# Second block's attention as one stage per layer: centred values, early rotation, gate logarithms under the retention, scores a head ahead

## The reference

```python
def retention_inputs(parts, rotate):            # 4 heads of 128
    q = to_heads(parts[0], 4) * 128 ** -0.5; k = to_heads(parts[1], 4)
    if rotate: q, k = rotary_2d(q, ...), rotary_2d(k, ...)      # latent tokens only
    v = to_heads(parts[2], 4)
    # one decay per head and direction: log1p(-exp(ret_decay))
def gla_inputs(parts):                          # 4 heads, keys of 64, values of 128
    a_f = log_sigmoid(parts[8] @ gate_up[0] + gate_b[0]) / 16   # a_b alike, with index 1

r_lat, r_ctx = bidirectional_scan(retention_inputs(lat, True), retention_inputs(cx, False))
g_lat, g_ctx = bidirectional_scan(gla_inputs(lat), gla_inputs(cx))
ret = from_heads(head_layernorm(r)) * silu(parts[3])   # minus mean, over root of variance, per head
gla = from_heads(rmsnorm(g, gla_norm_g)) * silu(parts[7])
x = x + g1 * (concatenate([ret, gla]) @ w_out)
```

## Time and profile before

| | |
|---|---|
| median of 3 runs | 2334.02 us (2332.15 to 2335.29) |
| profiled execution, its own time | 2339.86 us |
| span of the profiled execution | 2338.0 us |
| PE busy | 2096.0 us, 90% of the span |
| DVE, ACT, POOL busy | 707.7, 617.7, 267.7 us |
| granted TensorE clock, mean | 0.938 of full |

### The profile page before, as it was taken

How to read it: one execution, slowest core, us unless ns; L and a number is a source line. 1 busy time by engine, 2 the same in 40 slices (tenths; PEclk the granted TensorE clock), 3 DMA queues, 4 the chain that set the end, 5 groups by cost and what they waited for, 6 DMA issues and landing times. The chain is left out here.

```text
span 2338.0 us, 27789 instructions
## 1 busy us (share of the span) xinstructions
PE 2096.0 (90%) x11630; PEld 1465.7 (63%) x11630; DVE 707.7 (30%) x1250; ACT 617.7 (26%) x968; POOL 267.7 (11%) x121
## 2 busy tenths in 40 slices
PE   5999989989999999979975598999999797568998
PEld 2456787774444444458853446777777686358998
DVE  1103154222222222262333413222222533343333
ACT  1313112022222222231112314223332211334544
POOL 1000000010000000000000012323332000012663
PEclk9999978989999999989988699999999998769999
DMA  9276815257999999922230003343453134003441
GB/s 358 87 256 236 322 37 197 81 219 300 426 424 426 422 420 425 397 104 101 80 137 0 1 27 126 126 162 126 144 189 118 37 120 171 0 1 139 166 163 55
DMA packets 120207, 428.28 MB, mean 183 GB/s; under 512 B 5690, under 2 KB 23141, under 8 KB 107456
## 3 DMA queue, kind: packets, MB, share of 16 engines
q1 hardware_dynamic: 118016, 416.56, 46.4%
q0 software_dynamic: 2112, 10.56, 1.3%
HBM read 426.06 MB, written 1.05 MB: 183 GB/s over the span
## 5 line engine op out<-in xcount | busy, mean ns | idle before, releaser
L490 PE MATMUL bank<-arena_r,ring_low 128*128 128x512 f32 (+2 forms) x1696 | 533.1, 349 | 24.8 <-DVE H_low L1649 18.3
L490 PE MATMUL bank<-arena_r 128*128 128x512 f32 (+1 forms) x1792 | 510.6, 355 | 18.4 <-DVE H_low L1649 7.0
L490 PE MATMUL bank<-arena 128*128 128x64 bf16 (+9 forms) x2876 | 376.3, 308 | 56.4 <-ACT arena L1447 27.3
L490 PEld LDWEIGHTS bank<-arena_r 128*128 128x128 f32 x1792 | 316.9, 191 | 103.5 <-issue 45.2
L490 PEld LDWEIGHTS bank<-arena_r,ring_low 128*128 128x128 f32 (+1 forms) x1696 | 315.3, 191 | 69.3 <-issue 17.0
L490 PEld LDWEIGHTS bank<-arena 128*128 128x128 bf16 (+5 forms) x2876 | 243.1, 155 | 169.8 <-issue 140.6
L490 PE MATMUL bank<-ring,arena 128*64 128x512 f32 x1024 | 278.2, 595 | 0.4 <-DVE arena L1930 0.4
L1589 POOL TENSOR_TENSOR ring_low<-ring,arena_r 128x2048 fp32r<-128x2048 f32 x32 | 146.6, 4605 | 687.4 <-ACT arena_r L1494 687.4
L2131 DVE SCALAR_TENSOR_TENSOR X<-bank,mod,X 128x256 f32<-128x256 f32 x216 | 96.5, 481 | 327.0 <-PE bank L490 327.0
L490 PE MATMUL bank<-H,ring 128*128 128x256 f32 (+1 forms) x704 | 185.7, 423 | 0.5 <-issue 0.3
L490 PE MATMUL bank<-H_low,arena_r 128*128 128x512 f32 (+1 forms) x512 | 173.1, 338 | 0.0
(11 more groups left out here) (255 smaller groups left out, 1864.1 us busy)
## 6 DMA issues: line engine op xcount, KB each, us to landing
ring<-in_moe_w_gate SPq DMA_DIRECT2D x32, 2048.0 KB, 13.5
ring<-in_w_mlp SPq DMA_DIRECT2D x32, 2048.0 KB, 8.3
ring<-in_w_in SPq DMA_DIRECT2D x26, 2048.0 KB, 8.3
ring<-in_ada_w SPq DMA_DIRECT2D x24, 2048.0 KB, 11.9
ring<-in_moe_w_up SPq DMA_DIRECT2D x17, 2048.0 KB, 9.1
H<-in_moe_w_down SPq DMA_DIRECT2D x16, 2048.0 KB, 15.9
arena<-in_moe_w_up SPq DMA_DIRECT2D x15, 2048.0 KB, 9.2
ring<-in_moe_w_down SPq DMA_DIRECT2D x15, 2048.0 KB, 16.1
```

Of the source, the lines that this page charges most:

```text
L490: ins = nc.tensor.matmul(o, l, r, start=start, stop=stop, skip_group_check=True)
```

## The change

The three phases `ret`, `gf`, `gb` of a layer become one, `att`, and the order of the work in it is written anew for every engine.

- The swap matmuls of the rotation are issued after chunk 2 of the projection, and VectorE's rotation after the split of chunk 4.
- VectorE subtracts each head's mean from the values V during the projection (the layer norm's mean subtraction is linear in them), so the copy, the mean's ones-matmul and the subtraction of the retention's outputs are gone. Squares and products read the output banks directly.
- GpSimd makes the decay arguments, and clears the mask tiles.
- Decay buffers are in threes. Scores of head h + 1 are issued before the outputs of head h; the variance of head h - 1 after head h.
- Gate logits of both directions are made before the first head, and their logarithms and sums between the heads. The gate buffers are one per direction; the clearing of the output banks by matmuls is gone, the first matmul of each chunk starts the bank.
- The gated outputs are squared and scaled out of the banks without a copy; each head's square waits for that head.

```diff
@@ TensorE
                     chunk_used(2)
+                    if j == 2:
+                        flush()
+                        pe.wait_ge(S("b2_in"), 16 * (4 + l))
+                        pe.wait_ge(S("tile_free"), tiles[0] - 4)
+                        for m, M in enumerate((RQ, RK)):
+                            for h in range(RT_H):
+                                mm(ps[4 + m * 2 + h // 2][...], PERM, M[:, h, 0:L], inc="swapped" if h % 2 else None)
...
+                keys_turned(0)
+                for side in sides:
+                    scores(0, side)
+                for d in range(2):
+                    for t in range(2):
+                        mm(ps[(5, 1, 2, 3)[2 * d + t]], GUP[0:32, d, t * P:(t + 1) * P], DT[0:32, :], inc="gate_mm")
                 for h in range(RT_H):
+                    pe.wait_ge(S("rk_out"), c + 1)
                     pe.wait_ge(S("r_prep"), c + 1)
...
+                    if h:
+                        pe.wait_ge(S("gate_out"), 4 * l + h + 1)
                     for side in sides:
+                        pe.wait_ge(S("r_decayed"), q + 1)
+                        if h < RT_H - 1:
+                            scores(h + 1, side)
...
+                    pe.wait_ge(S("r_state_out"), c + 1)
...
+                    if h < RT_H - 1:
+                        keys_turned(h + 1)
+                    if h:
+                        pe.wait_ge(S("r_inverse" if h > 1 else "gate_out"), 4 * l + (h - 1 if h > 1 else 1))
+                        variance(h - 1, 5)
-                for h in range(4):
-                    mm(ps[h], GSC[:, 0, :], GSC[:, 0:4, :], True, False)
...
+                g_keys(0)
+                pe.wait_ge(S("r_normed"), 4 * l + 1)
+                variance(RT_H - 1, 0)
+                pe.wait_ge(S("r_inverse"), 4 * l + 3)
+                g_scores(0)
+                g_updates(0)
+                pe.wait_ge(S("r_normed"), 4 * l + 4)
+                g_intra(0)
+                g_keys(1)
+                pe.wait_ge(S("gq_ready"), 2 * (2 * l) + 2)
+                g_inter(0)
+                g_scores(1)
+                g_updates(1)
+                g_intra(1)
+                pe.wait_ge(S("gq_ready"), 2 * (2 * l + 1) + 2)
+                g_inter(1)
@@ ScalarE
                     if j == 6:
                         tables()
+                        head_exps(0)
...
+                keys_out(0)
+                gate_out(0)
+                head_exps(1)
+                state_out(0)
+                gate_soft(0)
+                keys_out(1)
+                gate_out(1)
+                head_square(0)
+                head_exps(2)
+                state_out(1)
+                gate_soft(1)
+                keys_out(2)
+                head_inverse(0, 5)
+                head_square(1)
+                head_exps(3)
+                state_out(2)
+                keys_out(3)
+                head_inverse(1, 5)
+                head_square(2)
+                state_out(3)
+                gate_exps(0)
+                head_inverse(2, 5)
+                head_square(3)
+                gate_keys(0)
+                head_inverse(3, 0)
+                gate_exps(1)
+                gate_keys(1)
@@ GpSimd
+                def head_args(h):
+                    G.tensor_scalar(w, EF, lf, None, ALU.mult)
+                    G.tensor_scalar(q, EB, lb_, None, ALU.mult).then_inc(S("r_arg"), 1)
+                    pool.wait_ge(S("r_arg"), c + 1)
+                    G.tensor_tensor(w, w, q, ALU.add).then_inc(S("r_arg"), 1)
+                    pool.wait_ge(S("r_arg"), c + 2)
+                    G.tensor_scalar(q[:, 0, :], ROWT[0], lf, None, ALU.mult)
+                    G.tensor_scalar(q[:, 1, :], ROWT[1], lb_, None, ALU.mult).then_inc(S("r_arg"), 1)
+                head_args(0)
+                phase_end(pool, f"l{l}_in")
+                head_args(1)
+                head_args(2)
+                pool.wait_ge(S("r_head"), RT_H * l + 1)
+                head_args(3)
+                for d, sem in enumerate(("r_head", "r_normed")):
+                    pool.wait_ge(S(sem), RT_H * l + 4)
+                    G.memset(GSC[d], 0.0).then_inc(S("gsc_clear"), 1)
@@ VectorE
+                dve.wait_ge(S("tile_free"), 48 + 29 * l + 12)
+                heads_of = RV.rearrange("p t (h v) -> p (t h) v", h=RT_H)
+                link(V.tensor_reduce(RMU, heads_of, AX.X, ALU.add))
+                V.scalar_tensor_tensor(heads_of, bc(RMU.unsqueeze(2), [P, 4 * RT_H, P]), -1.0 / P, heads_of, ALU.mult, ALU.add)
...
+                head_prep(0)
+                head_decay(0)
+                head_prep(1)
+                head_decay(1)
+                gate_sums(0)
+                head_prep(2)
+                head_decay(2)
+                head_norm(0)
+                gate_args(0)
+                head_prep(3)
+                head_decay(3)
+                head_norm(1)
+                gate_sums(1)
+                head_norm(2)
+                gate_products(0)
+                dve.wait_ge(S("r_head"), 4 * l + 4)
+                gate_args(1)
+                head_norm(3)
+                gate_queries(0)
+                gate_masks(0)
+                gate_states(0)
+                gate_products(1)
+                gate_queries(1)
+                gate_masks(1)
+                gate_states(1)
```

More of the change, by code:

```diff
@@ L1016, in _ @@
-                for d in range(2):
-                    g = 2 * l + d
-                    for t in range(2):
-                        mm(ps[4 + t], GUP[0:32, d, t * P:(t + 1) * P], DT[0:32, :], inc="gate_mm")
-                    pe.wait_ge(S("gke_ready"), g + 1)
+                            mm(ps[h][:, side * L:(side + 1) * L], RV[:, side * 2 + sblk, h * P:(h + 1) * P], RSC[i % 3][:, sblk, :],
+                               (side, sblk) == (0, 0), sblk == 1 and side == 1, inc="r_intra" if sblk else None)
@@ new lines, in gate_soft, with gate_exps @@
+                def gate_soft(d):
+                    act.wait_ge(S("gate_out"), 4 * l + 2 * d + 2)
+                    link(A_(GLg[d], GT1[d], ACT.Abs))
+                    link(A_(GLg[d], GLg[d], ACT.Exp, scale=-1.0))
+                    A_(GLg[d], GLg[d], ACT.Ln, bias=vec("one")).then_inc(S("g_soft"), 1)
+                def gate_exps(d):
+                    act.wait_ge(S("g_arg"), 2 * l + d + 1)
+                    A_(GKE[d], GKE[d], ACT.Exp, scale=1.0 / 16).then_inc(S("g_exp"), 1)
+                    link(A_(GKM[d], GT1[d], ACT.Exp, scale=-1.0 / 16))
+                    A_(GQM[d], GT1[d], ACT.Exp, scale=1.0 / 16).then_inc(S("g_exp"), 1)
```

328 lines of the change are left out of this document (153 added, 175 removed).

## The result

2195.3 us, median of 4 runs (2193.9 to 2201.4), against 2334.6 for the kernel before in the same session (2332.2 to 2335.3): ratio 0.9408, interval [0.9391, 0.9424], 139 us less. Run again it gave 0.9391 [0.9375, 0.9406]. The profiled execution took 2196.6 us (span 2194.7, mean granted clock 0.961).

The account below looks back on a forecast made before the run. No engine bounds the two stretches; they are chains of hand-overs. Gain 67.5 + 60.0 - 3, less 6 for hand-overs, is 118.5: 2339.9 becomes 2221.4 profiled, 2215 for the median; range 2200 to 2240.

Parts of the forecast that it names:

- what would show it: Signs for the forecast: stretches of 79 to 86 and 62 to 70 us, heads 8 us apart or less in layer 0.
- signs of being wrong: Heads staying 10.6 us apart, stretch clock under 0.7, or ScalarE waiting over 3 us for GpSimd at head 1.
- The walk: Step-by-step count of the new stage from its start: 78 us in layer 0, 58.2 in layer 1.
- GpSimd's term: Decay arguments made by GpSimd, ahead of ScalarE's exponentials: 1.5 us a layer, 3 in all (0 to 11).
- take off 6: Allowance on the summed gain for TensorE results reaching their readers 0.35 us late: 6 us (0 to 12).
- I add 4: Layer 1's stage: 4 us added to 58.2 because its heads ran partly at half clock.
- barrier: Between last projection matmul and stage: taking the tile, one small exponential and the barrier, 1.1 us for 9.9.
- the rest as it is: Outside the two stretches nothing changes but the place of some DVE and TensorE work in the projection.
- The own range: The forecast's own range, 2202 to 2230: below, no hand-over allowance and no GpSimd wait; above, both upper bounds.
- Heads coupled: Rival: written orders keep heads 10.6 us apart in both layers; 24 us less gain, 2239; chance 0.15.
- TensorE at 1.2 GHz: Rival: TensorE stays at half clock throughout the stages; 50 us less gain, 2265; chance 0.08.
- A very slow GpSimd: Rival: one-input scalar-column instructions before heads 1 to 3 very slow; at 6 us each, 2353; chance 0.02.

## Why the prediction was wrong, and where it was right

**The mechanism held.** Chains of hand-overs set the stretches, and their removal is the gain. Of the list of what would show it these were met: no clearing burst; swaps of 3.69 us behind chunk 2; layer 1's pause of 3.45 us in the projection gone (TensorE waits 1.1 us in all from 1790 to 1885); GpSimd's one-input 512-wide at 1.76 us, under 1.9; heads 7.8 us apart; one wait over 5 us before the masks. None of the signs of being wrong came: the clock was 0.91, ScalarE's longest wait for GpSimd 2.7 us. The first item was missed on the short side: the stretches took 77.6 and 58.4 us, and 79 to 86 and 62 to 70 had been put down.

**The walk came out within 2.2 us.** Layer 0, after its start: gate exponentials forecast at 28, measured 28.2; first masks done 45, 45.5; last burst's end 69.2, 67.9; `w_out` 78 without GpSimd's term, 76.8. Layer 1: gate exponentials 24.6, 26.8; first masks 39.3, 40.7; last burst's end 52.5, 52.0; `w_out` 58.2, 57.6. The swaps in layer 0 cost 4.0, forecast 4.4. Part of this is luck. Up to the gate exponentials the walk gave ScalarE 20.4 us of work and 7.4 of waits, with none for GpSimd:

```profile
1194.73:1222.97 28.24, 26.57 (x126) 20.28 (x127) 20.59 (x36) 18.66 (x32) 21.15 (x15) 1.00 0.61 221
```

It worked 18.7 us and waited 9.6, 3.5 of them for GpSimd, so the work and the other waits were both put too high, by 1.7 and 1.3 us, and GpSimd's waits made up for it.

**What failed is what was laid on top of the walk.** The sum took off 13 us in three allowances, and the measured times hold none of them:
- "A TensorE result reaches its reader some 0.35 us after its columns have gone; I counted that for some hand-overs only, and take off 6." The walk without it is not too short by the time of `w_out` in either layer. The likely reason is that rows with their pauses had been used for most steps, and such a row holds the hand-over already; that is argued.
- "The heads of this layer ran partly at half clock, so I add 4." Layer 1's stage came out 0.6 under the walk without them. Its first 12 us do run at 0.86 of the clock, but ScalarE's longest wait in them, 2.65 us, is for GpSimd and not for TensorE.
- GpSimd 3 us: ScalarE's waits for it are 3.5 and 5.5 us in the rows, and they lie inside the times that the walk met without them. So either they cost little, or the walk was too long by as much; no run here tells the two apart. The rule of the Trainium skill (GPSIMD Engine Reference, 4.1 Engine selection), weighed in the prediction, that one-input work runs there at roughly line rate, isn't borne out for this form: 1.76 us for 512 columns, where GpSimd's own two-input sum took 1.27 and VectorE's own product of that form, in the kernel before (line 2046), 0.48.

That is 13 of the 16 to 20 us between the forecast gain of 118.5 and the 134.9 to 138.2 of the profiles behind their start. The other 3.4 to 6.7 are: layer 0's stage 1.6 to 3.2 under walk and barrier, layer 1's 1.0, the swaps 0.4, the end of the program 2.6, less 0.4 to 2.1 that the stretch between the stages lost beyond the 1.0 counted there. At the end I had "the rest as it is", and layer 1's `w_out` now begins at full clock. Its first 10 us, before and then after:

```profile
2088.89:2098.89 10.00, 9.98 (x33) 8.32 (x34) 0.48 (x1) 4.13 (x3) 7.93 (x2) 0.71 0.00 0
```

```profile
1948.24:1958.24 10.00, 9.98 (x46) 8.82 (x47) 0.97 (x2) 4.55 (x4) 7.93 (x2) 1.00 0.00 0
```

33 records against 46 in the same time. The end as a whole doesn't follow from this stretch alone: with the pauses filled in both layers it begins at 1.00 too, and the end is 248.7 us long for 246.5.

**The range** failed with it, since its terms had room on one side only: every one of them could make the kernel slower than the walk, and none faster. The own range's lower end is said to be the sum with no hand-over allowance and no GpSimd wait; that is 2206.6. With all three allowances gone the sum gives 2339.9 - 127.5 - 4 - 5.8 = 2202.6, and there the own range ended. The last 7 us were in no bound.

**The rivals.** Heads coupled (0.15): their pace of 10.6 us did go, and the scores ahead are what removed it; where it is put back it costs 5 us a layer, so its time of 2239 was also too high. It counted from a first part of 30 us, where the walk has 28. TensorE at 1.2 GHz (0.08): the mechanism is real, as the late rotation shows, but the new order has no such wait at the head of the stage, and the clock reads 1.00 in its first 29 us. A very slow GpSimd (0.02): no, 1.76 us an instruction.

**Where the gain came from.** Of the 73.4 us that layer 0's stage lost, direction 1's preparation beside direction 0's is 20.3, the place of the gates 5.1 more on top of it, the early rotation 15.0 (11 net of the 4.0 that the swaps cost in the projection, and 7.7 of it clock), the scores ahead 5.0, the norms 0.3 to 1.9, each by undoing it. All but the gates' were undone singly, and parts can overlap, as direction 1 and the gates do. Some 27 us remain. The centring was 6.4 of them when done alone; that the clearing burst and its wait (6.7 and most of 7.8 us in the earlier trace rows) and the meetings of all engines between the old stages make up the rest is argued and wasn't tried.

## What to carry to other kernels

When the duration and pause of every step come from rows, look whether the hand-overs are in them already before adding an allowance, and give the range room on both sides: here three allowances of 13 us in all were too much, and every bound pointed the same way. Count what the clock does behind the changed stretch and not only in it. Before a part goes to a helper engine, work out its slack: here 3.3 us more in each of three sets cost 11 to 13 us a layer. And look in the trace where a moved instruction ran before reading a time from it.

## What the runs showed of the hardware that I had not expected

- A wait of 5.5 us in front of dense work cost more than itself: 44 records took 18.6 us behind it, 15.4 of them at a granted clock of 0.50, and 10.9 without it. With the wait filled by matmuls that nobody reads they took 14.2, and the clock fell to 0.50 in the middle of them, at about 1202.6, with no pause of over 0.8 us before.
- The start of the program, which no kernel here changes, runs now slower and now faster. The same 16 records take 1.92 or 3.64 us, and in six of the sixteen profiles 3.0 to 3.3. TensorE's timeline of the kernel before, and then of the changed kernel, at the same instruction:

```profile
38.13 3.64 PE L490 MATMUL bank<-ring,silc 128*32 128x512 f32 x16
```

```profile
37.31 1.92 PE L497 MATMUL bank<-ring,silc 128*32 128x512 f32 x16 [0.46 <-DMA ring<-in_ada_w]
```

  The granted clock of the stretch from 37 to 55 us reads 1.00 in both, so here the length of the records tells more than that column. The Trainium skill (TensorE: Matmul & The Clock Gate, What's actually happening) says that the count of slow matmuls at a kernel's start varies from run to run; the rows agree. Of the 8.4 us by which these two starts differ, 8.1 are there by the burst at 79.07 and 71.00 us. The starts of all profiles lie between 1017.1 and 1027.5 us, and in one session the kernel before shows two groups of times, 2331.0 to 2331.6 (6 runs) and 2339.7 to 2340.0 (3 runs). A difference of a few microseconds in medians of four runs is read from profiles with the start cut off.
- GpSimd's product with a scalar column: 1.76 us for 512 columns where its two-input sum of the same width takes 1.27. Beside VectorE's work single ones rose to 2.07 (1.56 with VectorE idle for most of it) and VectorE's scan from 2.34 to 2.73 us, its four scalings from 0.87 to 1.94.
